# K and the attention output kept token-major in DRAM and transposed by DMA, in a hybrid attention and gMLP step on eight cores

## The reference

```python
h = rmsnorm(x, norm_g)
z = h @ w_in                       # columns: q | k | v | f | g_A | u | v_B | g_B
q, k, v: 8 heads x 128;  logf = log_sigmoid(z_f + b_f)
att[t] = softmax_j<=t( q[t].k[j] * 128**-0.5 + sum_{j<i<=t} logf[i] ) @ v
out_a = att * silu(g_a)
out_b = gelu(u) * (W_s LN(gelu(v_B)) + b_s) * silu(g_b)
y = rmsnorm(x + concat(out_a, out_b) @ w_out)
```

## Time and profile before

| | |
|---|---|
| time, median of 3 | 1655.51 us (1655.28 to 1655.53) |
| time of the profiled execution | 1653.81 us |
| its span on the slowest core (core 6, role 0) | 1650.2 us |
| spans of the even cores | 1647.2 to 1650.2 us |
| spans of the odd cores | 1600.6 to 1606.0 us |
| busy on core 6: PE / DVE / ACT / POOL | 94% / 36% / 37% / 15% |
| DMA, share of 16 engines: GpSimd's queue / SP's queue | 28.7% / 26.9% |

### The profile page before, as it was taken

One profiled execution on the slowest core, in us unless ns is written; L12 is line 12 of the kernel. 1 busy time (PEld: TensorE's weight loads), 2 busy tenths in 40 slices (PEclk: granted clock), 3 DMA queues, 4 the chain that ended last, 5 costly groups with the idle time before them and its releaser, 6 DMA issues.

```text
span 1650.2 us, 32111 instructions; the slowest of 8 cores (1600.6 to 1650.2 us)
## 1 busy us (share of the span) xinstructions
PE 1543.8 (94%) x11687; PEld 909.4 (55%) x11687; DVE 599.1 (36%) x1252; ACT 603.5 (37%) x1191; POOL 246.3 (15%) x361
## 2 busy tenths in 40 slices
PE   3699999969999999999899999999999759999997
PEld 1365665534444444444478778678687634444443
DVE  1323332202444122332435445455455532333333
ACT  1223223212655322222226566566565651111111
POOL 5011111131333100000021211221111300000000
PEclk9899999989999999999999999999999889999999
DMA  9946455397000243433498868759736776645542
GB/s 190 213 143 195 150 192 162 122 175 103 6 1 1 26 54 42 53 43 56 54 174 87 112 79 118 108 70 122 104 58 102 137 170 215 202 154 204 192 152 94
DMA packets 236947, 191.38 MB, mean 116 GB/s; under 512 B 187498, under 2 KB 210194, under 8 KB 229266
## 3 DMA queue, kind: packets, MB, share of 16 engines
q0 software_dynamic: 141312, 54.57, 28.7%
q1 hardware_dynamic: 95474, 134.69, 26.9%
HBM read 182.94 MB, written 60.84 MB: 148 GB/s over the span
## 4 chain that ended last, share of the span: by engine, by line
PE 88%; DMA 5%; DVE 2%; issue 2%; ACT 2%; POOL 1%; POOLq 0%; DVEq 0%; ACTq 0%; SPq 0%
PE psb L589 24%; PE psb L1376 17%; PE psb L793 8%; PE psb L429 8%; PE psb L954 8%; PE psb L419 7%; PE psb L1251 5%; PE psb L1134 5%; DMA arena<-w_in 2%; DMA arena<-x_own 1%; DMA v_own<-arena 1%; POOL arena L122 1%; PE psb L1160 1%; PE psb L404 1%; PE psb L1145 1%
## 5 line engine op out<-in xcount | busy, mean ns | idle before, releaser
L589 PE MATMUL psb<-arena 128*128 128x496 bf16 (+1 forms) x1920 | 419.4, 372 | 3.2 <-ACT psb L803 2.8
L589 PEld LDWEIGHTS psb<-arena 128*128 128x128 bf16 x1920 | 183.9, 98 | 195.1 <-issue 6.3
L1376 PE MATMUL psb<-arena 128*128 128x512 bf16 (+1 forms) x1280 | 279.3, 382 | 9.8 <-DMA arena<-oT_s 9.8
L1181 ACT ACTIVATE arena<-psb,offb 128x384 bf16<-128x384 f32 x400 | 213.2, 580 | 57.8 <-PE psb L1134 44.9
L954 PE MATMUL psb<-arena 128*128 128x128 bf16 (+1 forms) x2560 | 217.8, 220 | 3.0 <-DVE arena L884 1.9
L1376 PEld LDWEIGHTS psb<-arena 128*128 128x128 bf16 (+1 forms) x1280 | 125.7, 98 | 163.2 <-issue 14.0
L1251 PE MATMUL psb<-arena 128*128 128x129 bf16 x1520 | 177.3, 221 | 5.3 <-POOL arena L1190 5.3
L1134 PE MATMUL psb<-arena 128*128 128x384 bf16 (+3 forms) x552 | 172.9, 314 | 7.1 <-ACT arena L1181 2.1
L954 PEld LDWEIGHTS psb<-arena 128*128 128x128 bf16 (+1 forms) x2560 | 166.0, 98 | 14.1 <-issue 3.2
L419 PE MATMUL psb<-arena 128*128 128x512 bf16 (+1 forms) x640 | 151.1, 396 | 15.9 <-DMA arena<-w_in 13.8
L429 PE MATMUL psb<-arena 128*128 128x344 bf16 (+1 forms) x960 | 146.9, 313 | 13.3 <-ACT arena L466 12.4
(11 more groups left out here) (157 smaller groups left out, 1201.1 us busy)
## 6 DMA issues: line engine op xcount, KB each, us to landing
arena<-x_own SPq DMA_DIRECT2D x38, 1024.0 KB, 7.9
y_own<-arena SPq DMA_DIRECT2D x19, 1024.0 KB, 4.8
arena<-w_in POOLq DMA_DIRECT2D x32, 512.0 KB, 6.5
k_own<-arena SPq DMA_DIRECT2D x19, 512.0 KB, 4.4
v_own<-arena SPq DMA_DIRECT2D x19, 512.0 KB, 3.6
arena<-w_in POOLq DMA_DIRECT2D x32, 256.0 KB, 11.3
arena<-ck POOLq DMA_DIRECT2D x16, 512.0 KB, 10.6
arena<-cv POOLq DMA_DIRECT2D x16, 512.0 KB, 7.9
```

Source lines behind the costliest of these rows:

```text
L589: PE.op(lambda: mm(PSB[bk][:, 0:n], wt[:, k, :], H[:, k, c0:c0 + n], start=(k == 0), stop=(k == KC - 1)), reads=rh + [r_wt], writes=[PSR[b ...
L1181: ACT.op(lambda: act(out=Pb[pi][:, 0:n], in_=PSB[bk][:, 0:n], func=AF.Exp, scale=SCALE, bias=S["offb"][:, t["oo"] + u["g"], h:h + 1]), rea ...
L1376: PE.op(lambda k=k, cg=cg, bk=bk: mm(PSB[bk][0:rows, :], oT[op_][:, k, j * 128:j * 128 + rows], wo[k][:, cg * 512:(cg + 1) * 512], start=( ...
```

## The change

K is stored as it is, token-major, in `K_s` [token, 1024], right after K's epilogue; it is no longer transposed in stage A. `e_loads` fetches a head's K with a transposing DMA on SP (2-byte elements, [tokens, 128] in DRAM to [128, tokens] in SBUF). The output of a tile is stored by `fin_out` into `o_s` [token, 1024], and the final stage fetches the attention half with a transposing DMA. The otr, smpT and nop units are gone, and with them the buffers KTsb, oTb and soT and the copies on VectorE. The spreading of the filler is written without its special cases. The gMLP half stays channel-major.

```diff
+    def dmat(self, out, in_, dsem, reads=(), writes=(), pwrites=()):
+        self._deps(reads, writes, pwrites)
+        self.eng.dma_start_transpose(out=out, in_=in_).then_inc(dsem.sem, 16)
...
-        self.KT_s = dscr("KT_s", [8, 128, NKEY + NRMAX], BF16)
+        self.K_s = dscr("K_s", [NKEY + NRMAX, 1024], BF16)
-        self.oT_s = dscr("oT_s", [16, 128, NOMAX * 128 + NRMAX], BF16)
+        self.oT_s = dscr("oT_s", [8, 128, NOMAX * 128 + NRMAX], BF16)
+        self.o_s = dscr("o_s", [NOMAX * 128 + NRMAX, 1024], BF16)
...
-        store(SP, C.KT_s.rearrange("h d t -> d h t")[:, :, tcol:tcol + rows], KTsb[p][:, :, 0:rows], R_KTsb[p], R_KTs)
+        store(SP, C.K_s[tcol:tcol + rows, :], Kb[p][0:rows, :], R_Kb[p], R_Ks)
...
-        if not todo:
-            a_KTtr(n); a_KTcopy(n); a_Kstores(n)
+        a_Kstores(n)
         for i, m in enumerate(todo):
...
             a_Vmm(m)
-            if i == 0:
-                a_KTtr(n)
             a_Vepi(m)
-            if i == 0:
-                a_KTcopy(n); a_Kstores(n)
             a_Vstores(m)
...
-        load(SP, KTh[p][:, 0:nk * 128], C.KT_s[h, :, 0:nk * 128], R_KTh[p], extra=[R_KTs])
+        tload(KTh[p][:, 0:nk * 128].unsqueeze(1), C.K_s[0:nk * 128, h * 128:(h + 1) * 128], R_KTh[p], extra=[R_Ks])
...
+        if a1 == t["nb"]:
+            store(SP, C.o_s[b0 * 128:(b0 + a1) * 128, h * 128:(h + 1) * 128].rearrange("(a t) c -> t a c", t=128), os_[o][:, 0:a1, :], R_os[o],
+                  R_oh[h][t["ti"]])
...
-        elif k == "otr":
...
-            for a in range(t["nb"]):
-                PE.op(lambda a=a: nc.tensor.transpose(PSB[bk][:, :].bitcast(BF16)[:, a * 128:(a + 1) * 128], os_[x][:, a, :], S["ident_b"][:, :]),
...
-            if u["pos"] >= 0:
-                fill_upto(-(-len(filler) * (u["pos"] + 1) // u["len"]) if u["pos"] < u["len"] - 1 else len(filler))
+            fill_upto(-(-len(filler) * (u["pos"] + 1) // u["len"]))
...
+            if half:
+                load(SP, oT[p][:, 8:16, 0:w], C.oT_s[:, :, b0 * 128:b0 * 128 + w].rearrange("k p t -> p k t"), R_oT[p][1], extra=R_oTg)
+            else:
+                tload(oT[p][:, 0:8, 0:w], C.o_s[b0 * 128:b0 * 128 + w, :], R_oT[p][0], extra=[R_oh[k][ti] for k in range(8) for ti in tis])
```

More of the change, by code:

```diff
@@ L126, in dma @@
         return ev
+    def dmat(self, out, in_, dsem, reads=(), writes=(), pwrites=()):
+        self._deps(reads, writes, pwrites)
+        self.eng.dma_start_transpose(out=out, in_=in_).then_inc(dsem.sem, 16)
+        dsem.cnt += 16
+        ev = (dsem.sem, dsem.cnt)
+        self._update(ev, reads, writes, pwrites)
+        return ev
 class Chip:
@@ L240, in pload, with tload @@
         return q.dma(out, in_, dsem_of(res), reads=list(extra), pwrites=[res])
+    def tload(out, in_, res, extra=(), part=False):
+        return SP.dmat(out, in_, dsem_of(res), reads=list(extra), writes=[] if part else [res], pwrites=[res] if part else [])
     def store(q, out, in_, res, dram_res=None):
@@ L286, in emit @@
     R_tz = [Res("tz%d" % i) for i in range(33)]
-    R_KTs, R_Vs, R_CQs = Res("KT_s"), Res("V_s"), Res("CQ_s")
+    R_Ks, R_Vs, R_CQs = Res("K_s"), Res("V_s"), Res("CQ_s")
     R_oTg = [Res("oT_g%d" % k) for k in range(8)]
-    R_oTh = [[Res("oT_h%d_%d" % (k, i)) for i in range(len(qtiles) + 1)] for k in range(8)]
+    R_oh = [[Res("o_h%d_%d" % (k, i)) for i in range(len(qtiles) + 1)] for k in range(8)]
     H, R_H, _ = place("H", 0, [KC, TO], BF16, parts=no + 1)
@@ L315, in emit @@
     Vb, R_Vb = b.many("Vb", 2, [1024], BF16)
-    KTsb, R_KTsb = b.many("KTsb", 2, [8, 128], BF16)
     R_ss = [Res("ss%d" % i) for i in range(2)]
@@ L386, in emit @@
     psT = [PSB[i][:, :].bitcast(BF16).rearrange("p (k t) -> p k t", k=8) for i in range(2)]
-    psKT = PSB[7][:, :].bitcast(BF16).rearrange("p (h t) -> p h t", h=8)
     def a_norm(n):
@@ L448, in a_Kepi @@
             pool(lambda: g.tensor_copy(out=Kb[p][0:rows, :], in_=Kf[0:rows, :]), reads=[R_Kf], writes=[R_Kb[p]])
[L450 to L457, removed]
     def a_Vepi(n):
@@ L473, in a_Vepi @@
             pool(lambda: g.tensor_copy(out=Vb[p][0:rows, :], in_=Vf[0:rows, :]), reads=[R_Vf], writes=[R_Vb[p]])
[L475 to L478, removed]
     def a_Kstores(n):
@@ L888, in mixing @@
                    reads=[R_t1[u], R_GB[p]], writes=[R_ob[p]] if ti == 0 else [], pwrites=[] if ti == 0 else [R_ob[p]])
-        store(SP, C.oT_s[8 + gi, :, 0:TO], ob[p][:, :], R_ob[p], R_oTg[gi])
+        store(SP, C.oT_s[gi, :, 0:TO], ob[p][:, :], R_ob[p], R_oTg[gi])
     EB = W0 + 2 * QS + 2 * QS + 4096 + 512
@@ L921, in e_loads @@
         p = h % 2
-        load(SP, KTh[p][:, 0:nk * 128], C.KT_s[h, :, 0:nk * 128], R_KTh[p], extra=[R_KTs])
+        tload(KTh[p][:, 0:nk * 128].unsqueeze(1), C.K_s[0:nk * 128, h * 128:(h + 1) * 128], R_KTh[p], extra=[R_Ks])
         if ns:
-            pload(SP, KTh[p][:, nk * 128:nk * 128 + NR], C.KT_s[h, :, NKEY:NKEY + NR], R_KTh[p], extra=[R_KTs])
+            tload(KTh[p][:, nk * 128:nk * 128 + NR].unsqueeze(1), C.K_s[NKEY:NKEY + NR, h * 128:(h + 1) * 128], R_KTh[p], extra=[R_Ks], part=True)
         first = True
@@ L984, in emit @@
     os_, R_os = b.many("os", 3, [4, 128], BF16)
-    oTb, R_oTb = b.many("oTb", 3, [512], BF16)
     if ns:
@@ L994, in emit @@
         sob, R_sob = b.take("sob", [128], BF16)
-        soT, R_soT = b.many("soT", 2, [NR], BF16)
         for i in range(ns):
@@ L1027, in emit @@
     ring_load()
-    LADD, LPV, LACC, LTR = 3, 5, 7, 12
+    LPV, LACC = 5, 7
     units = []
@@ L1044, in emit @@
             for pos, kd, i in ((0, "ktc0", 0), (1, "ktc1", 0), (8, "smpS", 0), (14, "smpO", 0),
-                               (36, "ktc0", 1), (37, "ktc1", 1), (44, "smpS", 1), (50, "smpO", 1), (60, "smpT", 1)):
+                               (36, "ktc0", 1), (37, "ktc1", 1), (44, "smpS", 1), (50, "smpO", 1)):
                 hu.insert(pos, dict(kind=kd, h=h, st=i))
@@ L1052, in emit @@
         units.extend(hu)
[L1053 to L1066, removed]
     NU = len(units)
@@ L1164, in e_S @@
                       reads=[R_Vh[p], R_Pn], pwrites=[PSR[bk]])
-        elif k == "smpT":
-            PE.op(lambda: nc.tensor.transpose(PSB[bk][:, :].bitcast(BF16)[:, 0:NR], sob[0:NR, :], S["ident_b"][0:NR, 0:NR]),
-                  reads=[R_sob, R["ident_b"]], writes=[PSR[bk]])
     def e_soft(i):
@@ L1191, in e_soft @@
                                              fill=0.0, base=0, channel_multiplier=-1), reads=[R_Pb[pi]], writes=[R_Pb[pi]])
[L1192 to L1197, removed]
         elif k in ("ktc0", "ktc1"):
@@ L1230, in e_soft @@
                                                       op0=ALU.mult, op1=ALU.mult), reads=[R_so, R_GAh[p]], writes=[R_sob])
-        elif k == "smpT":
-            DVE.op(lambda: v.tensor_copy(out=soT[p][:, :], in_=PSB[bk][:, :].bitcast(BF16)[:, 0:NR]), reads=[PSR[bk]], writes=[R_soT[p]])
-            store(SP, C.oT_s[h, :, no * 128:no * 128 + NR], soT[p][:, :], R_soT[p], R_oTh[h][len(qtiles)])
+                store(SP, C.o_s[no * 128:no * 128 + NR, h * 128:(h + 1) * 128], sob[0:NR, :], R_sob, R_oh[h][len(qtiles)])
     def e_PV(i):
@@ L1347, in g_load @@
         for half in (1, 0):
-            ex = R_oTg if half else [R_oTh[k][ti] for k in range(8) for ti in tis]
-            load(SP, oT[p][:, half * 8:(half + 1) * 8, 0:w],
-                 C.oT_s[half * 8:(half + 1) * 8, :, b0 * 128:b0 * 128 + w].rearrange("k p t -> p k t"), R_oT[p][half], extra=ex)
+            if half:
+                load(SP, oT[p][:, 8:16, 0:w], C.oT_s[:, :, b0 * 128:b0 * 128 + w].rearrange("k p t -> p k t"), R_oT[p][1], extra=R_oTg)
+            else:
+                tload(oT[p][:, 0:8, 0:w], C.o_s[b0 * 128:b0 * 128 + w, :], R_oT[p][0], extra=[R_oh[k][ti] for k in range(8) for ti in tis])
     fbl = []
```

3 lines of the change are left out of this document (removed).

## The result

The changed kernel takes 1618.3 us (median of 4), the kernel before took 1655.4 beside it. The ratio is 0.9776 [0.9757, 0.9795]: 37 us faster. One of the four executions fell in the chip's slower state (1740 us) and does not enter the ratio. The profiled execution took 1617.8 us. The median lies 5 us above the forecast of 1613.

A forecast was written before the change was run, and what follows sets the result against it. PE, busy 94% of the span, was taken as the bound. 7.5 + 12 + 13 + 12 - 2 = 42.5 us off the profiled 1653.8 gives 1611.3; the runs' median lies 1.7 higher, so 1613 us, range 1600 to 1642.

The forecast's parts named there:

- start: Start of stage A: without small-piece K stores ahead, block 3's x lands some 11 us sooner; 12 us gained, bounds 0 and 15.
- K's transposes: Stage A: taking K's transposes off PE saves 0.45 us a step over 17 steps, 7.5 us.
- end of stage A: Without the small-piece K store ahead of v_own, PE's 11.5 us wait and cold clock go; 13 us, bounds 0 and 14.
- attention's transposes: Attention: 152 output blocks at 56 ns leave PE, 8.5 us, plus waits and the shorter end chain; 12 us together.
- final stage: Start of final stage: the transposed attention half lands at 1371.2, due at 1368.9, costing 2 us.
- a sign against me: Attention: waits of L1186 for CQ were listed among the signs that the prediction is wrong.
- The transposing loads: K in 7.0 us and the half in 11.8, priced as 256-byte pieces; K hidden, the first half costs 2 us.
- Rival 2: Transposed pieces cost twice or so: K's 14 us stays hidden, the final half lands 14 us late; 1627 us, chance 0.11.
- rival 3: Transposing loads hold up SP's queue at head 0, later heads and final stage: 113 us, about 1725; chance 0.15.
- the cover of 20 us: Head 0: from K's issue at 829.7 to first scores at 850.0; K and V loads were expected hidden within it.
- Not checked off: Listed signs of being right: early PE waits at most 2 us, v_own under 7, K loads under 12; wrong: long SP issues.

The follow-up runs named there:

- e3: Changed kernel, but stage A still transposes K on TensorE and copies it on VectorE, with nothing reading the copy: 1625.6 us, ratio 0.9831.
- e4: Kernel before, but transposed K stored block by block in 2 KB pieces and fetched by plain loads, all transposes still on TensorE: 1635.5 us, ratio 0.9893.
- e11: Changed kernel, with fin_acc one unit earlier, 6 in place of 7 units behind the scores: 1611.0 us, ratio 0.9742.
- e5: Changed kernel, with each head's transposing K load done twice, the second after the first has landed: 1629.7 us, ratio 0.9853.
- e14: Changed kernel, with each head's K load doubled and head 0's first two CQ rows issued ahead of its K and V: 1629.1 us, ratio 0.9839.
- e6: Changed kernel, with the final stage reading the gMLP half again by plain load in place of the attention half's transposing load: 1620.2 us, ratio 0.9798.

## Why the prediction was right

The forecast was 1613 (range 1600 to 1642) and faster at 0.82; it came out at 1618.3. Nearly all steps fell a little short, and only the 2 us of the last went the other way, so it was not right by errors that cancelled. Step by step, in us gained:

| step | predicted | measured |
|---|---|---|
| start | 12 (0 to 15) | 11.2 on core 6, 10.6 on the mean |
| K's transposes | 7.5 | 6.7 for 15 blocks, 7.3 by e3 |
| end of stage A | 13 (0 to 14) | 11.2 on core 6, 10.6 on the mean |
| attention's transposes | 12 | 9.2 |
| final stage | -2 | 0 |

*The start.* Right in place, cause and, to 1 or 2 us, in size. x landed 9.3 us sooner, K ran at full clock, and the weights of V were next late, as written: PE waits 1 to 2.5 us for them within block 0 on three of the four even cores.

*K's transposes.* Right: 0.45 us a block, and e3 gives the same, within its interval, by putting them back.

*The end of stage A.* The cause was right, shown by e4. The size was off by 2 us, in one term: "v_own's 128 rows should land in 4 to 6 us". They took 8.1, over the 6.9 us of the next V block, so 1.6 us of wait stayed; and on core 0 the granted clock fell for the next block (0.66 from 335 to 340 us), which took 8.54 us instead of 6.87. No small store is ahead of v_own any more, and it still takes twice the median of 3.6 us: that the weights of GpSimd's queue hold it up that much fits, but no run here took them away.

*Attention.* The term "They replace no wait, as L1251 and filler matmuls follow at once" was right for the transposes: PE's busy time fell by 12.3 us, more than the 8.5 written. What failed is the premise that nothing comes in their place. With the otr units gone, `fin_acc` is written further on in the filler, and g_A's epilogue on VectorE came to stand before it: 7.9 us of new waits. The prediction has no term for this, and does not ask who waits behind the epilogue. e11 gets 7 of them back. At the end of attention 1.1 us was written for the missing transposes and copy, and 0.6 came. And in the last head a CQ row stands behind output stores and costs 2 us (L1213 for L1156), the wait of the old L1186 that was listed as a sign against me.

*The transposing loads.* I took 7.0 us for K and 11.8 for the half; they took 4.9 to 12.1 and 12.5. The half came 4 us before its use, not 2 after: it landed 5.8 us behind the first half, where its whole 11.8 had been put behind it. Rivals 2 and 3 had both priced it too high. (Rival 2's own sum counts the 2 us of the forecast twice: 14 us late makes 1625, not 1627.) But the claim "If the cover of 20 us is passed, PE stands" was made for K and V alone. CQ's rows stand behind them and are due as soon. K itself landed 15 us ahead of the first scores (803.2 + 5.1 against 823.2, where their weights are loaded), but the first CQ row had 3.7 us, and e5 and e14 show that doubling the load, still under the "three times" from which rival 3 was to decide, costs 11 us. The forecast for head 0 was right by less than it believed.

*Not checked off.* PE's wait at 66 us was 2.27, over the 2 written, since VectorE scales H late. v_own took 8.1 us and not under 7, and one K load of eight took 12.1 and not under 12. SP's issues of transposing DMAs did last many us (3 to 6 for K, 8 to 13 for a half), which I had listed as a sign of being wrong. It is one only where something behind them is due.

## What to carry to other kernels

When a transfer is late, look at what stands ahead of it in its queue, and count its pieces, not its bytes: stores of 1024 small pieces cost here more than all of K's transposes, and storing the same in larger pieces gave 18 us with every transpose kept. When a unit of work is taken out of an interleaved list, what is written a fixed number of units later moves against everything spread over that list; reread afterwards which engine has what ahead of the operation that frees a bank. And price a load by everything that stands behind it in its queue until the next deadline, not by its own deadline.

## What the runs showed of the hardware

- A transposing DMA on SP's queue fetched K, 19 blocks of 128x128 in bf16, in 4.9 to 12.1 us, and 1 MB per group in the final stage in 11.4 to 15.5 (core 0 of after). In e6 the plain loads of 1 MB there, three of them one behind another, took 17.2 at the median.
- Its issue holds SP for 2.9 to 5.6 us for K and for 7.6 to 13.4 for a half (core 0 of after). The K loads of head 0 hold it for 15.7 us in e5 and 19.7 in e14, where the second of two also waits for the first to land. K's plain load took 1.03 us to issue, a CQ row that stood alone 0.3 to 0.5. What stands behind it is issued that much later, however small it is.
- Small pieces on the way out have a price too. A tile's output was stored in 128 rows of 768 bytes, and is now stored in 384 of 256. Beside w_out's loads in the last head the stores land in 12.0 us at the median, before in 7.6 (core 6, 1288 to 1363 us), and the CQ rows between them in 13.8, before in 7.5. DMA issues, 1255 to 1330 us, core 0 of after:

```profile
arena<-w_out POOLq DMA_DIRECT2D x16, 512.0 KB, 23.4
...
arena<-CQ_s SPq DMA_DIRECT2D x4, 192.0 KB, 13.8
o_s<-arena SPq DMA_DIRECT2D x7, 96.0 KB, 12.0
```
